# Modulation sums in PSUM, a new place for the input sums, and another order in the short down part

## The reference

```python
def adaln(cond, w, b):
    m = jax.nn.silu(cond) @ w + b
    return m.reshape(cond.shape[0], 1, N_MOD, D_MODEL)

def modulate(x, g, shift, scale):
    return rmsnorm(x, g) * (1.0 + scale) + shift

def swiglu(x, wg, wu, wd):
    return (jax.nn.silu(x @ wg) * (x @ wu)) @ wd

def ffn_half(x, m, j, g, wg, wu, wd):
    return x + 0.5 * m[:, :, j + 2] * swiglu(modulate(x, g, m[:, :, j], m[:, :, j + 1]), wg, wu, wd)
```

## Time and profile before

| | |
|---|---|
| median of 3 runs | 2727.3 us (2726.56 to 2728.72) |
| profiled execution | 2727.09 us, span 2725.6 us |
| mean granted TensorE clock | 0.98 |
| PE busy | 2568.2 us, 94% |
| DVE busy | 1917.7 us, 70% |
| ACT busy | 1064.7 us, 39% |
| POOL busy | 1019.1 us, 37% |
| phases, by the timeline | ffn0 to 550, even mixer to 947, ffn1 to 1444, ffn2 to 1929, odd mixer to 2249, ffn3 to 2712 |

### The profile page before, as it was taken

One profiled execution on the slowest core, in us unless ns is written; L12 is line 12 of the kernel. 1 busy time (PEld: TensorE's weight loads), 2 busy tenths in 40 slices (PEclk: granted clock), 3 DMA queues, 4 the chain that ended last, 5 costly groups with the idle time before them and its releaser, 6 DMA issues. The chain is left out here.

```text
span 2725.6 us, 43019 instructions
## 1 busy us (share of the span) xinstructions
PE 2568.2 (94%) x17283; PEld 2465.5 (90%) x17283; DVE 1917.7 (70%) x2907; ACT 1064.7 (39%) x1740; POOL 1019.1 (37%) x671
## 2 busy tenths in 40 slices
PE   6999999899989998999989899999999999899998
PEld 5999999899766998898989798999999999899998
DVE  6897798725677697778778877776564569756473
ACT  4221122243665553333335342424532555334343
POOL 3454455343200343424344342534442224442433
PEclk8999999999999999999999899999999999899999
DMA  7443543431100221424224133322321222122222
GB/s 275 151 134 120 175 144 110 138 105 49 57 1 1 93 93 62 138 65 139 78 95 138 47 113 105 113 89 86 96 63 55 66 82 93 47 93 78 78 74 74
DMA packets 205075, 259.88 MB, mean 95 GB/s; under 512 B 4965, under 2 KB 160233, under 8 KB 204905
## 3 DMA queue, kind: packets, MB, share of 16 engines
q1 hardware_dynamic: 204232, 254.88, 28.2%
q10 hardware_dynamic: 672, 2.62, 0.3%
HBM read 253.66 MB, written 3.82 MB: 94 GB/s over the span
## 5 line engine op out<-in xcount | busy, mean ns | idle before, releaser
L2469 POOL TENSOR_TENSOR wl<-raw,wh 128x512 fp32r<-128x512 f32 (+1 forms) x440 | 665.4, 1542 | 921.3 <-ACT wh L2582 856.6
L2582 ACT CAST wh<-raw 128x2048 fp32r<-128x2048 f32 (+2 forms) x122 | 210.6, 1726 | 549.4 <-PE psU L3326 427.4
L2897 DVE SCALAR_TENSOR_TENSOR macc<-mraw,cs,macc 128x512 f32<-128x512 f32 x448 | 396.4, 952 | 2.4 <-DMA mraw<-in_mod_w 2.4
L2519 POOL TENSOR_TENSOR wl<-raw,wh 128x512 fp32r<-128x512 f32 x54 | 84.0, 1556 | 458.7 <-ACT wh L2722 458.7
L3322 PE MATMUL psU<-hh,wh 128*128 128x386 f32 (+1 forms) x896 | 207.2, 312 | 2.7 <-issue 2.7
L3322 PE MATMUL psG<-hh,wh 128*128 128x386 f32 x880 | 206.7, 316 | 1.1 <-DVE hl L3293 1.1
L3326 PE MATMUL psU<-hh,wl 128*128 128x386 f32 (+1 forms) x896 | 206.0, 311 | 0.0
L3324 PE MATMUL psU<-hl,wh 128*128 128x386 f32 (+1 forms) x896 | 205.5, 310 | 0.0
L3326 PE MATMUL psG<-hh,wl 128*128 128x386 f32 x880 | 202.9, 312 | 0.0
L3324 PE MATMUL psG<-hl,wh 128*128 128x386 f32 x880 | 202.4, 311 | 0.0
L3322 PE MATMUL psG<-ah,wh 128*128 128x384 f32 (+1 forms) x560 | 135.0, 323 | 54.1 <-issue 29.5
(11 more groups left out here) (680 smaller groups left out, 7095.9 us busy)
## 6 DMA issues: line engine op xcount, KB each, us to landing
mraw<-in_mod_w SPq DMA_DIRECT2D x64, 1024.0 KB, 6.2
raw<-in_ffn_w_gate SPq DMA_DIRECT2D x44, 1024.0 KB, 5.2
raw<-in_ffn_w_up SPq DMA_DIRECT2D x44, 1024.0 KB, 5.1
raw<-in_ffn_w_down SPq DMA_DIRECT2D x44, 768.0 KB, 4.3
raw<-in_odd_w_in SPq DMA_DIRECT2D x12, 1024.0 KB, 5.1
raw<-in_even_w_in SPq DMA_DIRECT2D x9, 1024.0 KB, 5.1
raw<-in_ffn_w_down SPq DMA_DIRECT2D x6, 1024.0 KB, 6.6
raw<-in_ffn_w_down SPq DMA_DIRECT2D x8, 640.0 KB, 4.1
```

The lines of the kernel that those rows point to most:

```text
L2469: ins = nc.gpsimd.tensor_tensor(wl[:, slot, piece], raw[:, slot, piece], wh[:, slot, piece].bitcast(F32), ALU.subtract)
L2519: nc.gpsimd.tensor_tensor(part3(f, wl, 5), quarter(n, 1, 1), part3(f, wh, 5).bitcast(F32), ALU.subtract).then_inc(block_plo, 1)
L2582: nc.scalar.copy(wh[:, slot, 0:width], raw[:, slot, 0:width]).then_inc(w_hi, 1)
L2897: ins = nc.vector.scalar_tensor_tensor(out=macc[:, c], in0=mraw[:, s, k], scalar=scalar, in1=macc[:, c], op0=ALU.mult, op1=ALU.add)
```

## The change

- `MOD_PLAN` has six entries for a `seven_ffn`: for each of the three parts one for its units and one for its down part. ffn1 has (2, 4, 2, 4, 2, 2), ffn2 (2, 4, 2, 2, 2, 2), ffn3 none. The head pairs carry none any more. ffn0 keeps its plan.
- `mod_sum` accumulates in `psA` and `psB`; only the last step of a pair of units writes `macc` in SBUF. It can do a stretch of its 8 steps (`first`, `last`). It waits for `mred_ok`, and in ffn0's first pair it stands behind the wait for `rms_ok`.
- `mod_turn` is 8 matmuls with `macc` as weights and the one column `one` as the moving operand, into 8 columns of `psA`. `mod_reduce` is only the addition of the bias.
- In the units of a part `unit_mods` does two steps ahead of line 3141 and two at the unit's end, in units 1 to 4. The turn stands behind unit 5. In the down part the first two modulation units are summed at the start of rounds 0 and 1 with the turn behind tile (1, 1), and where there are four, the other two at the end of rounds 2 and 3 with the turn behind tile (3, 1).
- `sum_f` lies in the buffer of `mraw` (three of the sums) and in `zf` (the fourth). All eight `input_rows` and `input_high` and the four `input_sum` stand in the first head pair, GpSimd's `zl` too.
- In the short down part each `input_sum_lo` is followed by a residual, and the later blocks and residuals alternate.

The plan and the buffers:

```diff
-MOD_PLAN = {0: (12, 6, 10, 6), 1: (4, 0, 4, 4, 2), 2: (4, 0, 4, 4, 0), 3: (4, 0, 0, 0, 0)}
+MOD_PLAN = {0: (12, 6, 10, 6), 1: (2, 4, 2, 4, 2, 2), 2: (2, 4, 2, 2, 2, 2), 3: (0, 0, 0, 0, 0, 0)}
...
-    sum_f, _ = view("sum_f", [P, 4, QUAD], at, end_h)
+    sum_m, _ = view("sum_m", [P, 3, QUAD], at_m, end_m)
+    sum_f = [sum_m[:, 0], sum_m[:, 1], sum_m[:, 2], zf[:, 0, 1]]
```

SyncE's program:

```diff
+                    if j == 1 and plan[2 * part - 2]:
+                        if part == 1:
+                            sp.wait_ge(sum_lo, 4 * f)
+                        for s in range(2):
+                            modulation(2 * part - 2, 0, s)
```

GpSimd's, in the head pairs:

```diff
+                if i == 0:
+                    pool.wait_ge(zh_ok, DT * f)
+                    pool.wait_ge(sum_ok, 4 * f)
+                    for kh, h in ((0, 0), (1, 0), (1, 1)):
+                        nc.gpsimd.tensor_tensor(zl[:, kh, h], zf[:, kh, h], zh[:, kh, h].bitcast(F32),
+                                                ALU.subtract).then_inc(zl_ok, 1)
```

ScalarE's, in the head pairs:

```diff
-                for k in range(4 * i, 4 * i + 4):
-                    input_high(k)
+                if i == 0:
+                    for k in range(DT):
+                        input_high(k)
```

VectorE's: the step, the reduction, the units, the short and the long down part:

```diff
+        def mod_sum(q0, i, s, first=0, last=MOD_STEPS):
+
+            if first == 0:
+                dve.wait_ge((mred_ok, macc_ok)[s], (i * 2) + (q0 + s))
+                dve.wait_ge(mod_in[s], (i * 16) + ((q0 - MOD_HEAD) // 2 * 16 + 16))
+            for step in range(first, last):
+                k, c = step // 2, step % 2
+                scalar = cs[:, s * MOD_K + k, c:c + 1]
+                acc = (psA, psB)[c][:]
+                if s == 0 and k == 0:
+                    st.mark(nc.vector.tensor_scalar(acc, mraw[:, s, k], scalar, None, ALU.mult))
+                    continue
+                if k:
+                    st.wait(back=1)
+                out = macc[:, c] if s == 1 and k == MOD_K - 1 else acc
+                ins = nc.vector.scalar_tensor_tensor(out=out, in0=mraw[:, s, k], scalar=scalar, in1=acc, op0=ALU.mult, op1=ALU.add)
...
-            for c in range(2):
-                ins = nc.vector.tensor_reduce(mred[:, c], (psA, psB)[c][:].rearrange("p (t b) -> p t b", b=P), AX.X, ALU.add)
...
-            nc.vector.tensor_tensor(mod[:, :, col], mred[:],
+            nc.vector.tensor_tensor(mod[:, :, col], psA[:, 0:8].rearrange("p (c t) -> p c t", c=2),
...
+                unit_mods(part, 4 * j)
                 dve.wait_ge(seven_mm, 7 * u + 5)
...
+                unit_mods(part, 4 * j + 2)
+
+            def unit_mods(part, step):
+
+                step -= MOD_STEPS // 2
+                if plan[2 * part - 2] and 0 <= step < 2 * MOD_STEPS:
+                    mod_sum(MOD_BASE[f, 2 * part - 2], 0, step // MOD_STEPS, step % MOD_STEPS, step % MOD_STEPS + 2)
...
-            dve.wait_ge(zh_ok, DT * f)
-            dve.wait_ge(up_mm, old_tiles(f) + HEAD_TILES)
-            for s in range(4):
-                input_sum(s)
-                residual(s // 2, s % 2, rb)
             for s in range(4):
                 input_sum_lo(s)
+                residual(s // 2, s % 2, rb)
             first_low(1, 0)
             first_sums(1, 0)
             residual(2, 0, rb)
             sum_lows(1, 0, 2)
             sum_lows(1, 0, 3)
             residual(2, 1, rb)
+            third_sum(1, 0)
             residual(3, 0, rb)
+            sum_lows(1, 0, 4)
             residual(3, 1, rb)
-            third_sum(1, 0)
-            sum_lows(1, 0, 4)
...
+                if plan[2 * part - 2]:
+                    mod_reduce(MOD_BASE[f, 2 * part - 2])
+                q0, mods = MOD_BASE[f, 2 * part - 1], plan[2 * part - 1]
                 for i in range(4):
+                    if i < 2 and mods:
+                        mod_sum(q0, 0, i)
                     for m in range(2):
                         residual(i, m, rb)
                         if part == N_PARTS:
                             z_low(r + 1, i, m)
+                        if i == 2 and m == 0 and mods:
+                            mod_reduce(q0)
+                    if i >= 2 and mods > 2:
+                        mod_sum(q0, 1, i - 2)
```

TensorE's:

```diff
-                    ins = turn((psA, psB)[c][:, t * P:(t + 1) * P], macc[:, c, t * P:(t + 1) * P])
+                    ins = nc.tensor.matmul(psA[:, 4 * c + t:4 * c + t + 1], macc[:, c, t * P:(t + 1) * P], one, start=True, stop=True)
...
+                if plan[2 * part - 2]:
+                    mod_turn(MOD_BASE[f, 2 * part - 2])
...
-                        if m == 0 and i and 2 * (i - 1) < mods:
-                            mod_turn(MOD_BASE[f, 1 + part], i - 1)
+                        if m == 1 and i % 2 and i - 1 < mods:
+                            mod_turn(MOD_BASE[f, 2 * part - 1], i // 2)
```

More of the change, by code:

```diff
@@ L2421, in down @@
                               w_down[:, k0:k0 + PART_TILES, f, i * PAIR:(i + 1) * PAIR])
-                mods = plan[1 + part]
+                mods = plan[2 * part - 1]
                 for i in range(4):
                     down(i)
-                    if i >= 1 and 2 * (i - 1) < mods:
+                    if i == 1 and mods:
                         for s in range(2):
-                            modulation(1 + part, i - 1, s)
+                            modulation(2 * part - 1, 0, s)
+                    if i >= 2 and mods > 2:
+                        modulation(2 * part - 1, 1, i - 2)
         for name in phases:
@@ L2883, in _ @@
         st = Steps(dve, dve_steps)
[L2885 to L2889, removed]
-                for c in range(2):
[L2891 to L2902, removed]
+        def mod_sum(q0, i, s, first=0, last=MOD_STEPS):
[13 more added lines that the diff above has]
+                ins = nc.vector.scalar_tensor_tensor(out=out, in0=mraw[:, s, k], scalar=scalar, in1=acc, op0=ALU.mult, op1=ALU.add)
+                if step == MOD_STEPS - 1:
+                    ins.then_inc(macc_ok, 1)
+                else:
+                    st.mark(ins)
         def mod_reduce(q0, i=0):
@@ L2997, in turn @@
                             t = i * 2 + (FT * f + 2 * pair0)
+                            if part == 0:
+                                dve.wait_ge(rms_ok, r + 1)
                             if carries:
                                 mod_sum(q0, i, 0)
-                            if part == 0:
-                                dve.wait_ge(rms_ok, r + 1)
                             passed(dve, prod_ok, t)
@@ L3078, in input_sum_lo @@
                 dve.wait_ge(sum_hi, 4 * (f - 1) + s + 1)
-                nc.vector.tensor_tensor(sum_l[:, s], sum_f[:, s], sum_h[:, s].bitcast(F32), ALU.subtract).then_inc(sum_lo, 1)
+                nc.vector.tensor_tensor(sum_l[:, s], sum_f[s], sum_h[:, s].bitcast(F32), ALU.subtract).then_inc(sum_lo, 1)
             def first_low(part, j):
@@ L3167, in seven_ffn @@
                     ins.then_inc(g_scaled, 1)
[L3168 to L3171, removed]
+                if i == 0:
+                    for k in range(DT):
+                        input_rows(k)
                 dve.wait_ge(a_lo, FT * f + 2 * i)
@@ L3185, in seven_ffn @@
                     ins.then_inc(prod_ok, 1)
-                if carries:
-                    mod_reduce(MOD_BASE[f, 0], i)
+                if i == 0:
+                    dve.wait_ge(zh_ok, DT * f)
+                    for s in range(4):
+                        input_sum(s)
             rb = res_base[f, 0]
             gate_of(l * N_MOD + (2 if j2 == 0 else 8), 0.5, rb)
-            dve.wait_ge(zh_ok, DT * f)
-            dve.wait_ge(up_mm, old_tiles(f) + HEAD_TILES)
-            for s in range(4):
-                input_sum(s)
-                residual(s // 2, s % 2, rb)
             for s in range(4):
                 input_sum_lo(s)
+                residual(s // 2, s % 2, rb)
             first_low(1, 0)
```

44 lines of the change are left out of this document (11 added, 33 removed).

## The result

The changed kernel takes 2757.7 us (median of 4 runs, 2752.09 to 2760.66), 30.6 us more than the 2727.1 of the kernel before: a ratio of 1.0112, 95% interval 1.0099 to 1.0125. The direction was forecast and the range (2715 to 2765) holds it, but +14 was forecast and +30.6 came. Its four runs also lie 8.6 us apart, where those of before span 2.2.

A forecast was written before the change was run, and what follows sets the result against it. TensorE, busy for 94% of the span, was taken as the bound, with large waits from VectorE being late. Terms 16 - 35 + 28 + 5 = +14 on 2727.09 us gave 2741 us, range 2715 to 2765.

The forecast's parts named there:

- The turn: ffn0's 17 turns: 8 one-column matmuls, 16 records, 1.8 us, +1.0 each; +16 in sum, bounds 12 and 25.
- Rival (e): All turns: no dearer, because a column of one would be a single record; -25, 2716 us; chance 0.05.
- The step: VectorE's modulation step with its sum in PSUM: 0.66 us start to start, never stretched; bounds 0.55 and 1.0.
- Rival (d): VectorE's PSUM steps: 1.0 us each, in units, down parts and ffn0 part 3; near 2789 us; chance 0.06.
- The units: Units 2 and 4 of six parts: added steps delay last_product, TensorE waits 2.3 us 12 times; +28, bounds 0 and +44.
- Heads and short parts: Head pairs and short down parts of three FFNs: 11.6 us returned each; -35 in sum, bounds -42 and -24.
- tile 6 waits no more: Short down parts: early sums, with sum_l and residuals alternating, end TensorE's wait at tile 6; 11.6 us returned per FFN.
- Long down parts: Down parts of ffn1 and ffn2: 62 to 64 us of waits and turns replaced by 69; +5, bounds -6 and +20.
- The rest: Even, odd, ffn3's parts and the end: 0 forecast.
- rival (c): Heads: return only 4 us each instead of 11.6, as GpSimd's chain wl, zl, wl ends late; 2764 us; chance 0.12.

The follow-up runs named there:

- residuals first: The changed kernel with residual(3, 0) and residual(3, 1) of the short down part ahead of third_sum again: 2742.3 us.
- the old turn: The changed kernel with the kernel before's 8 transposes into two PSUM banks and two VectorE reductions for each turn: 2739.6 us.
- the late turn: The changed kernel with the second turn of three down parts moved behind unit 0 of the next part: 2756.9 us; third_sum moved ahead came in a later run.
- mending three places: The changed kernel with modulation steps moved out of up units 1 and 3, residuals ahead of third_sum, and transposes with reductions: 2701.4 us.

## Why the prediction was half right

- **The turn**, ffn0: right (+16, measured +15.5; 1.8 us against 1.70). Rival (e), a single record for each column, is out.
- **The step**: right in length and in not being stretched. Rival (d) is out.
- **The units**: mechanism, place and number of waits right, 2.06 us against 2.3. Mis-sized was what a wait costs beyond itself. The prediction has "waits below 2.8 us lost mostly only themselves"; here 4 of 12 waits of 2.06 and all three of 1.83 lost 1.5 us more, and the trace of before had the low level behind two of its three waits of 1.82. The term was 28 and is 32.9.
- **Heads and short parts**: this is the step that failed. "tile 6 waits no more" was right, but I followed the residuals only to `residual(2, 0)` and not to the end of the new order, where `third_sum` waits for the last tile with `residual(3, 0)` behind it. That lost 3.6 us three times: 2.1 ahead of unit 0, which is in this term, and 1.5 of low clock behind its start, which the table puts to the parts. The term was -35 and is -30.2; with the residuals first it is -38.9, or -36.4 without the low clock that was missing there, so the other heads' terms held within 1.4 us together.
- **Long down parts**: the three waits behind tile (3, 1) were 7.8 us against 8.1. Less the units' 32.9, and the 3.0 of low clock behind `third_sum`'s waits in ffn1 and ffn2, the 42.2 leave +6.3, where I had +5. Inside it the turn behind a wait was wrong, 3.43 us and not 1.8 in five places.
- **The rest**: even, odd, ffn3's parts and the end gave +1.9 where I had 0. 1.5 of them are the low clock behind ffn3's wait for the residual; the mixers have no edit.

So 15.5 - 30.2 + 42.2 + 1.9 = 29.4, the profiled executions' difference, against 16 - 35 + 33 + 0 = 14. Of the 15.4 that are missing, 10.7 are `third_sum` ahead of `residual(3, 0)` (shown, by undoing it; that is three waits of 2.1 and 4.5 us of the 1.2 GHz level behind them), 4.9 are the units (6.0 us of that level behind four waits, less the 0.1 us by which each wait was shorter than forecast), and the other differences cancel to -0.2. The medians add 1.3. That the time lies inside the range is luck: the range reached to 2765 for rival (c), which is not what happened (the heads returned 10 us each, not 4). That the low level follows a wait of 2 us in some cases is in each of the four traces that have these waits; why in these and not in others stays open. The same units with the same waits had it behind 4, 2, 10 and 6 of the twelve (the changed kernel, residuals first, the old turn, the late turn). It may be why the runs of one kernel lie 8.6 us apart, but that is only argued: no run removes the level and keeps the waits.

## What to carry to other kernels

When an order written out by hand is changed, follow each engine to the end of the new order and ask of every operation with a wait who stands behind it: `third_sum` made two thirds of the miss by standing one line too early, and the late turn gained nothing until the same operation was moved out of its way, and then stopped at the next one, `last_sum`. Cost a small operation that two engines exchange as a round trip and at the low clock, if it stands behind a wait. And take a change of many parts apart before judging it: here the sums in PSUM alone gave 16 us, the new turn alone cost 60, and mending three places turned +30.6 into -26.2.

## What the hardware did that I had not expected

- Contention of a step with GpSimd falls on one of the two, and not always the same. In the kernel before, eight steps that started at 1291.87 took 5.38 us and GpSimd's three operations from 1291.88 took 9.00; with the new turn, eight from 1316.67 took 8.45 and GpSimd's three from 1317.17 4.75. With the operand in PSUM no step of 448 took over 0.757 us. The Trainium skill ("GPSIMD Engine Reference", section Specifications) says that VectorE and GpSimd contend where VectorE's instruction has two SBUF inputs; by that rule a step with one operand in PSUM is free of it, and the traces agree (0.757 us at most, where the two-SBUF step went to 2.057).
- A one-column f32 matmul takes 0.107 us from record to record, two records each, at the 2.4 GHz level and 0.21 at 1.2 GHz, so a turn of 8 takes 1.70 or 3.43 us, although it streams eight columns.
